# A two-layer streaming encoder step: the norm's column factor moves from the feed-forward operands to the evacuations

## What is computed

```python
def _rmsnorm(x, g):
    xf = x.astype(jnp.float32)
    y = xf * lax.rsqrt(jnp.mean(xf * xf, axis=-1, keepdims=True) + EPS)
    return (y * g.astype(jnp.float32)).astype(x.dtype)

for l in range(DEPTH):                               # DEPTH = 2
    h = _rmsnorm(x, p['norm_mix'][l])
    if l % 2 == 0:                                   # HGRN2 and retention heads
        z = (h @ p['w_in0'][a]).astype(f32)
        ...
        x = x + mix @ p['w_out0'][a]
    else:                                            # mLSTM
        up = (h @ p['w_up1'][c]).astype(f32)
        xm, zg = jnp.split(up, 2, axis=-1)           # zg only enters as silu(zg), at the end
        ...
        x = x + (hC * jax.nn.silu(zg)).astype(x.dtype) @ p['w_down1'][c]
    h = _rmsnorm(x, p['norm_ffn'][l])
    x = x + (jax.nn.silu(h @ p['w_ffn_gate'][l]) * (h @ p['w_ffn_up'][l])) @ p['w_ffn_down'][l]
y = _rmsnorm(x, p['norm_final'])
```

## Time and profile before

| | |
|---|---|
| time, median of 3 runs | 2166.68 us (2166.18 to 2167.81) |
| the profiled execution's own time | 2165.86 us |
| its span, first to last instruction | 2164.1 us |
| mean granted clock of TensorE | 0.979 of full speed |
| TensorE busy | 2062.3 us, 95% of the span |
| VectorE busy | 879.3 us, 41% |
| ScalarE busy | 430.5 us, 20% |
| GpSimd busy | 914.9 us, 42% |

### The profile page before, as it was taken

How to read it: one execution, slowest core, us unless ns; L and a number is a source line. 1 busy time by engine, 2 the same in 40 slices (tenths; PEclk the granted TensorE clock), 3 DMA queues, 4 the chain that set the end, 5 groups by cost and what they waited for, 6 DMA issues and landing times.

```text
span 2164.1 us, 33587 instructions
## 1 busy us (share of the span) xinstructions
PE 2062.3 (95%) x13453; PEld 1876.2 (87%) x13453; DVE 879.3 (41%) x1118; ACT 430.5 (20%) x671; POOL 914.9 (42%) x580
## 2 busy tenths in 40 slices
PE   6999999889999999989999999999899999999997
PEld 5999988789999999989998746547498999999996
DVE  4565645552222001359932356555722322210125
ACT  3242333221111000121212322323201111100011
POOL 4333323154454454555553123223454454455443
PEclk9999999899999999999999999999999999999998
DMA  4121212112222222232232474765822122222222
GB/s 172 59 86 60 85 57 84 43 57 78 73 72 78 78 68 78 81 137 75 84 121 75 142 268 145 258 208 186 297 88 78 59 68 77 78 72 75 78 77 88
DMA packets 82071, 224.35 MB, mean 104 GB/s; under 512 B 6352, under 2 KB 11344, under 8 KB 81232
## 3 DMA queue, kind: packets, MB, share of 16 engines
q1 hardware_dynamic: 73344, 202.94, 27.7%
q10 hardware_dynamic: 8656, 20.39, 2.6%
HBM read 170.06 MB, written 53.25 MB: 103 GB/s over the span
## 4 chain that ended last, share of the span: by engine, by line
PE 84%; DVE 8%; DMA 3%; ACT 3%; issue 1%; POOL 1%; DVEq 0%; SPq 0%; ACTq 0%; POOLq 0%
PE psd L210 11%; PE psd L214 11%; PE psd L215 11%; PE psd L211 11%; PE psd L217 11%; PE psd L216 11%; DVE ntmp L284 2%; PE psm L389 2%; PE psm L1314 2%; PE psd L1210 1%; PE psd L1199 1%; DMA c_s<-CsB 1%; PE psd L1136 1%; DMA CsB<-st_c 1%; PE psm L1299 1%
## 5 line engine op out<-in xcount | busy, mean ns | idle before, releaser
L1897 POOL CAST whi<-wraw 128x1024 fp32r<-128x1024 f32 x223 | 236.1, 1059 | 916.6 <-PE psd L217 486.7
L1899 POOL TENSOR_TENSOR wlo<-wraw,whi 128x1024 fp32r<-128x1024 f32 x223 | 540.6, 2424 | 17.9
L210 PE MATMUL psd<-xh,whi 128*128 128x320 f32 x1280 | 406.3, 317 | 19.9 <-ACT xh L257 14.1
L214 PE MATMUL psd<-xl,whi 128*128 128x320 f32 x1280 | 402.7, 315 | 9.5 <-POOL xl L292 7.5
L211 PE MATMUL psd<-xh,whi 128*128 128x320 f32 x1280 | 398.8, 312 | 0.0
L215 PE MATMUL psd<-xl,whi 128*128 128x320 f32 x1280 | 398.8, 312 | 0.0
L216 PE MATMUL psd<-xh,wlo 128*128 128x320 f32 x1280 | 398.5, 311 | 0.0
L217 PE MATMUL psd<-xh,wlo 128*128 128x320 f32 x1280 | 398.3, 311 | 0.0
L210 PEld LDWEIGHTS psd<-xh,whi 128*128 128x128 f32 x1280 | 243.2, 190 | 24.3 <-issue 23.6
L214 PEld LDWEIGHTS psd<-xl,whi 128*128 128x128 f32 x1280 | 242.9, 190 | 17.9 <-POOL xl L292 13.1
L211 PEld LDWEIGHTS psd<-xh,whi 128*128 128x128 f32 x1280 | 243.5, 190 | 0.8 <-issue 0.2
(11 more groups left out here) (378 smaller groups left out, 2902.8 us busy)
## 6 DMA issues: line engine op xcount, KB each, us to landing
wraw<-w SPq DMA_DIRECT2D x224, 512.0 KB, 3.3
CsA<-st_c SPq DMA_DIRECT2D x7, 1024.0 KB, 6.2
CsB<-st_c SPq DMA_DIRECT2D x7, 1024.0 KB, 8.8
c_s<-CsA SPq DMA_DIRECT2D x7, 1024.0 KB, 6.0
c_s<-CsB SPq DMA_DIRECT2D x7, 1024.0 KB, 8.8
z_kept<-zb ACTq DMA_DIRECT2D x16, 320.0 KB, 2.2
ztp<-st_c SPq DMA_DIRECT2D x5, 1024.0 KB, 7.8
CsC<-st_c SPq DMA_DIRECT2D x5, 1024.0 KB, 8.2
```

Source lines behind the costliest of these rows:

```text
L210: pe.matmul(o0, wh, x0, start=st, stop=False)
L214: pe.matmul(o0, wh, l0, start=False, stop=False)
L1897: pool.tensor_copy(whi[s][:], wraw[s][:]).then_inc(w_high, 1)
L1899: pool.tensor_tensor(wlo[s][:], wraw[s][:], whi[s][:].bitcast(F32), ALU.subtract).then_inc(w_split, 1)
```

## The change

The residual stream is no longer normed ahead of the two feed-forward layers. Instead, while the projection before still runs, each finished tile of `xT` is multiplied with the gain alone and split in high and low ("raw" operands); gate and up are projected from those, and VectorE multiplies the gate result and the SiLU with the column factor at the evacuation. The norm's matmuls against ones run in the middle of the first unit, into another PSUM tensor. The hidden tiles use half of `ah` and `al`, since raw operands use the other half, so they are made in three parts (8, 8, 6).

In the projection up, the last four gate tiles (`Z_RAW`) come first, from raw operands; VectorE multiplies them with the factor, and meanwhile makes the scaled operands for the other 28 units. `Z_FIRST` falls from 10 to 6. GpSimd no longer makes low parts for these norms. The additions behind the output projection now wait on VectorE for the last stores of the head states.

```diff
-FF_PARTS = (16, 6)
+FF_PARTS = (8, 8, 6)
...
@@ class Norm, act
                     a.wait_ge(*self.x_at(k))
+                    if self.raw is not None:
+                        a.activation(self.raw[0][:, k, :], xT[:, k, :], ACT.Copy,
+                                     scale=par[:, self.gain + k:self.gain + k + 1]).then_inc(self.raw_hi, 1)
...
+            def low_raw(self, v, k):
+                if self.raw is None:
+                    return
+                v.wait_ge(self.raw_hi, k + 1)
+                one = lambda x: x[:, bass.ds(k, 1), :].rearrange("p a c -> p (a c)")
+                v.scalar_tensor_tensor(one(self.raw[1]), one(xT), par[:, bass.ds(self.gain + k, 1)],
+                                       one(self.raw[0]).bitcast(F32), ALU.mult, ALU.subtract)\
+                    .then_inc(self.raw_lo, 1)
...
+            def scaled(self, v, ks):
+                for k in ks:
+                    if k >= 4:
+                        v.wait_ge(*self.ready(k - 4))
+                    v.scalar_tensor_tensor(ntmp[k % 4][:], xT[:, k, :], par[:, self.gain + k:self.gain + k + 1],
+                                           rstd[:], ALU.mult, ALU.mult).then_inc(self.v_done, 1)
+                    if k:
+                        self.low(v, k - 1)
...
@@ class MLstm
-        Z_FIRST = 10
+        Z_FIRST = 6
+        Z_RAW = 4
+            def raw_gate(self, a, j):
+                g, s = G_UP1 + j, j % 2
+                a.wait_ge(evac[g % 2], g // 2 + 1)
+                if j >= 2:
+                    a.wait_ge(self.zst[s], 16 * (j // 2))
+                a.activation(fft[s][:], ffs[s][:], ACT.Silu).then_inc(self.zr, 1)
+                a.wait_ge(self.zr, j + 1)
+                a.dma_start(io["z_kept"][CI - Z_RAW + j], fft[s][:]).then_inc(self.zst[s], 16)
+            def raw_gate_scaled(self, v, j):
+                g, s = G_UP1 + j, j % 2
+                v.wait_ge(pe_unit, U_UP1 + j + 1)
+                if j >= 2:
+                    v.wait_ge(self.zr, j - 1)
+                v.tensor_tensor(two(ffs[s][:]), psd[g % 2][:, :, 0:HT], two(rstd[:]), ALU.mult).then_inc(evac[g % 2], 1)
...
             def vec(self, v):
-                v.wait_ge(self.w_in, 80)
-                v.wait_ge(pe_unit, U_UP1)
+                v.wait_ge(norm2.std_done, 2)
+                norm2.scaled(v, [0])
+                self.raw_gate_scaled(v, 0)
+                norm2.scaled(v, range(1, KD))
+                norm2.low(v, KD - 1)
+                for j in range(1, Z_RAW):
+                    self.raw_gate_scaled(v, j)
+                v.wait_ge(self.w_in, 64)
+                v.wait_ge(pe_unit, U_UP1 + Z_RAW)
...
             def pe(self, pe):
+                for j in range(Z_RAW):
+                    first = j == 0
+                    pe_dense(pe, (U_UP1 + j, 0), (G_UP1 + j, 0), *raw1, ready=norm2.ready_raw if first else None,
+                             ready_high=norm2.ready_raw_high if first else None,
+                             between=(lambda: norm2.pe(pe)) if first else None)
...
@@ vec_residual
                 v.tensor_tensor(x, x, psd[(g0 + s) % 2][:, :, 0:HT], ALU.add).then_inc(evac[(g0 + s) % 2], 1)
                 if norm is not None:
+                    norm.low_raw(v, 2 * i + s)
                     norm.add(v, 2 * i + s, s)
...
@@ class FeedForward, act
-                            a.activation(two(ffs[s][:]), psd[gg % 2][:, :, 0:HT], ACT.Silu).then_inc(evac[gg % 2], 1)
+                            a.activation(ffs[s][:], ffg[s][:], ACT.Silu).then_inc(self.silu, 1)
...
@@ class FeedForward, vec
+                            v.wait_ge(pe_unit, u + 4 * i + 2 * s + 1)
+                            v.tensor_tensor(two(ffg[s][:]), psd[gg % 2][:, :, 0:HT], two(rstd[:]), ALU.mult)\
+                                .then_inc(evac[gg % 2], 1)
+                            v.wait_ge(self.silu, n + 1)
+                            v.tensor_tensor(ffs[s][:], ffs[s][:], rstd[:], ALU.mult).then_inc(self.scaled, 1)
...
@@ class FeedForward, pe
-                        pe_dense(pe, (u + j, 0), (g + j, 0), xh, xl,
-                                 ready=self.norm.ready if before == 0 and j == 0 else None,
-                                 ready_high=self.norm.ready_high if before == 0 and j == 0 else None)
+                        pe_dense(pe, (u + j, 0), (g + j, 0), *self.x,
+                                 ready=self.norm.ready_raw if first else None,
+                                 ready_high=self.norm.ready_raw_high if first else None,
+                                 between=(lambda: self.norm.pe(pe)) if first else None)
...
@@ SyncE
-            stream(U_UP1, U_DN1)
+            stream(U_UP1, U_UP1 + Z_RAW, 2 * CI - Z_RAW)
+            stream(U_UP1 + Z_RAW, U_DN1, -Z_RAW)
...
@@ GpSimd
-            splits(2, U_FF0 + 2)
-            norm1.pool(pool)
-            splits(U_FF0 + 2, U_UP1 + 2)
-            norm2.pool(pool)
-            splits(U_UP1 + 2, U_DN1)
+            splits(2, U_DN1)
...
@@ VectorE
             low(7, 8)
+            v.wait_ge(a_out, 32 * H)
+            v.wait_ge(b_out, 32 * H)
             vec_residual(v, (U_OUT0, 1), G_OUT0, norm1)
-            norm1.vec(v)
             ffn0.vec(v)
-            norm2.vec(v)
             mlstm.vec(v)
```

More of the change, by code:

```diff
@@ L224, in trunk, with __init__ @@
         class Norm:
-            def __init__(self, name, gain, g, free_at, x_at, final=False, own_sum=False):
+            def __init__(self, name, gain, g, free_at, x_at, final=False, own_sum=False, raw=None, again=False):
                 self.own_sum = own_sum
+                self.raw, self.again = raw, again
+                self.raw_hi, self.raw_lo = sem(f"{name}_raw_hi"), sem(f"{name}_raw_lo")
                 self.sq_done = sem(f"{name}_sq")
@@ L246, in act @@
                 a.wait_ge(self.sum_done, 1)
-                a.activation(two(rstd[:]), psd[self.g % 2][:, :, 0:HT], ACT.Ln, bias=eps,
+                o = psd[self.g % 2][:, :, 0:HT] if self.raw is None else psm[:, 0:2, 0:HT]
+                a.activation(two(rstd[:]), o, ACT.Ln, bias=eps,
                              scale=1.0 / D).then_inc(self.std_done, 1)
@@ L913, in conv_tile @@
                     ins.then_inc(self.conv, 1)
+            def raw_gate(self, a, j):
[12 more added lines that the diff above has]
+                v.tensor_tensor(two(ffs[s][:]), psd[g % 2][:, :, 0:HT], two(rstd[:]), ALU.mult).then_inc(evac[g % 2], 1)
             def act(self, a):
+                norm2.high(a, [0])
+                self.raw_gate(a, 0)
+                norm2.high(a, range(1, KD))
                 a.wait_ge(norm2.v_done, KD)
@@ L973, in act @@
                     a.dma_start(io[dst], src[:]).then_inc(self.outs, 16)
-                for i in range(Z_FIRST // 2 + 1, CI // 2):
+                for i in range(Z_FIRST // 2 + 1, (CI - Z_RAW) // 2):
                     for s in range(2):
@@ L1811, in parts @@
                 for f in FF_PARTS:
-                    nu = -(-f // KD)
-                    yield f, before, u, g, nu
-                    u, g, before = u + 2 * f + KD * nu, g + 2 * f + KD, before + f
+                    yield f, before, u, g
+                    u, g, before = u + 2 * f + KD, g + 2 * f + KD, before + f
             def act(self, a):
-                for f, before, u, g, nu in self.parts():
+                for f, before, u, g in self.parts():
                     with a.Fori(0, f // 2) as i:
@@ L1841, in vec @@
                                 .then_inc(self.lo, 1)
-                    vec_residual(v, (u + 2 * f, nu), g + 2 * f, self.after if before else None)
+                    vec_residual(v, (u + 2 * f, 1), g + 2 * f, self.after if before + f == sum(FF_PARTS) else None)
             def pe(self, pe):
-                for f, before, u, g, nu in self.parts():
+                for f, before, u, g in self.parts():
                     for j in range(4):
-                        pe_dense(pe, (u + j, 0), (g + j, 0), xh, xl,
-                                 ready=self.norm.ready if before == 0 and j == 0 else None,
-                                 ready_high=self.norm.ready_high if before == 0 and j == 0 else None)
+                        first = before == 0 and j == 0
+                        pe_dense(pe, (u + j, 0), (g + j, 0), *self.x,
+                                 ready=self.norm.ready_raw if first else None,
+                                 ready_high=self.norm.ready_raw_high if first else None,
+                                 between=(lambda: self.norm.pe(pe)) if first else None)
```

116 lines of the change are left out of this document (65 added, 51 removed).

## The result

The changed kernel takes 2138.01 us, the median of four runs (2133.3 to 2138.48), beside 2166.43 for the kernel before (2161.24 to 2167.81): a ratio of 0.9868, 95% interval 0.9847 to 0.989, so 1.3% faster. The forecast was 2142, with a range of 2132 to 2149. The profiled execution took 2138.1 us (span 2136.3), 27.8 us of span less than the one before.

The account below looks back on a forecast made before the run. TensorE's queue, busy 95% of the span, was taken as the bound. Gains of 11.5, 11.4 and 1.4 us (11.4 - 8 - 2 in the projection up) sum to 24.3, giving 2142 us, range 2132 to 2149.

Parts of the forecast that it names:

- The norm's terms: At the two feed-forward boundaries, all of the norm's cost but its sum on TensorE goes: 11.5 and 11.4 us gained.
- The wait in the projection up: Ahead of the fourth gate unit, TensorE waits for VectorE's late evacuation of the second: 7 to 8.9 us, taken as 8.
- the lower clock: Behind the hole in the projection up, TensorE runs some 4 us mostly at 1.2 GHz: 2.0 us lost.
- that case: In the projection up, GpSimd's casts block VectorE as well as its subtractions: evacuation at 32.3, a stall of 8.9 us.
- the three parts: In the feed-forward layers, eight more residual additions per layer, 0.82 us each on VectorE, and no more matmuls: cost nothing.
- the feed-forward loop's products: Two more VectorE operations per pair; the gate's chain takes 4.5 us against 7.04 until the next unit: cost nothing.
- the convolution behind the gate tiles: Behind the projection up's first four gate tiles, 8 of 36 us of cover stay ahead of the gates' matmuls: cost nothing.
- the additions behind the state stores: At the output projection, residual additions wait on VectorE behind the last state stores: 0 to perhaps 1 us, taken as 0.
- The first, no stall: In the projection up, VectorE slips between the splits or TensorE isn't held: gain 34.3 us, time 2132; chance 0.10.
- The weight split as the bound: VectorE's new products hold up GpSimd's weight split by 0.82 us for each of 44 pairs: 36 us, 2178; chance 0.04.
- the late raw pieces: Raw pieces come late, the first unit crawls as before and the change doesn't take effect: about 2166; chance 0.03.

Follow-up runs that it names:

- the reordered version with the load moved: Changed kernel with VectorE's gate evacuations moved between the scalings, and ScalarE's `wgx` load moved behind the first two `xm` evacuations: 2128.11 us, ratio 0.9832.

## Why the prediction was right

- **The norm's terms.** 11.5 and 11.4 were forecast, 11.8 and 11.6 came. The difference is the sum on TensorE, 2.15 us in place of 2.3, and in the first layer 0.05 us for eight faster steps. The cover was there: `ah` and `al` of the last tile were done in time, the factor too, and TensorE waits for neither.
- **The wait in the projection up.** Forecast: TensorE wants to begin gate 3 after 23.4 us and can between 30.4 and 32.3, so 7 to 8.9, taken as 8, and 2.0 at the lower clock. Measured from 927.36: wanted at 23.3, begun at 31.0, a hole of 7.74, and 2.25 at the lower clock. But the price of 8 was right by luck: two errors against each other. The casts do block, 1.9 us for the three (1.9 forecast for that case), and that speaks for 8.9; VectorE's free pairs came every 1.53 us where 1.66 had been counted, 1.0 less for the fifteen, and the subtractions blocked 6.5 where 6.75 had been counted. 8.9 - 1.0 - 0.2 = 7.7; what else differs (a start 0.3 us sooner, TensorE's own start 0.15 us behind the evacuation's end) about cancels.
- **The rule beside it** (the Trainium skill, "SBUF — State Buffer", Who interferes with whom: a VectorE operation with two SBUF inputs contends with a GpSimd operation that reads SBUF, for an exclusive lock). The trace agrees for the casts too, with the rows of 1.66 and 1.65. By that rule the prediction had a stall of 8.9; what that has too much is mainly VectorE's own pace.
- **What was put at nothing** was nothing: the three parts (0.9991), the feed-forward loop's products (0.6 us in a layer with four more per pair), the convolution behind the gate tiles (no wait of TensorE between the hole and the gates' matmuls, 1122.59), the additions behind the state stores (the head is 1.3 us longer, and no wait of TensorE for L1860 stands in its list).
- **The rivals.** The first, no stall, didn't occur. Its price can be held against the reordered version with the load moved, which has no stall: 2128.11, where 2132 was worked out; 2.6 of the 3.9 between are the first layer's paces of the k steps. The weight split as the bound and the late raw pieces didn't occur.
- **What was missed:** 2.6 us of faster k steps in the first feed-forward layer. The prediction took a matmul's duration as a constant; the two paces stood in the trace of before, in the stretches on `xh` and on `ah`, and the change's move of operands from one to the other was a term of the sum. The rest of the 4 us between forecast and median is within the spread of the runs.

## What to carry to other kernels

A factor that is one number per column can leave the operands and come back at the evacuation; what it frees is the whole chain between two projections, and what stays is the sum itself. Where the freed time is filled by work on another engine, count that engine's queue up to the evacuation that the bounding engine needs, with the lock against its neighbour in the count, and put the evacuations between the long work rather than behind it. When one wait is removed, look for the next on the same queue before you believe the gain: here a load that waited for stores came up some 20 us later.

## What the runs showed of the hardware

- Six matmuls of 320 columns take 880.0, 877.8 or 873.3 ns at the full clock, by where the low operand lies from the high one: 880.0 at a multiple of 2048 bytes, 877.8 at 128 and at 1664 bytes beyond one, 873.3 at 64 and at 1728. The two that give 873.3 are odd multiples of 64 and the others even ones; no more is shown of the rule. It doesn't hold alone: in five of the versions a stretch whose two parts kept their distance took 880.0 where it had taken 873.3, in one of them with nothing moved in SBUF, and a stretch at 880.0 in the kernel before took 873.3 in two. What decides that stays open.
- An operation on two SBUF tensors on VectorE and GpSimd's cast or subtraction held each other up, in both directions: 0.81 became 3.02 beside a subtraction, 1.65 beside a cast, and the cast of 1.04 became 1.65, the subtraction of 2.4 became 2.86.
- After a hole of 7.74 us TensorE's next three k steps ran at a granted clock of 0.51, so at about the lower of its two levels, 1.2 GHz, and the fourth at the full one.
